# State pass with token rows of two blocks loaded in place of TensorE transposes; last head's PSUM banks and closing weights in another order

## What is computed

```python
proj = x @ w_in                       # split into q_g, k_g, v_g, g_g, gk_lo, q_s, k_s, v_s
gk   = log_sigmoid(gk_lo @ w_gk2 + b_gk) / 16
gla  = gated_linear_attention(q_g, k_g, v_g, gk)   # 4 heads, dk 128, dv 256, recurrent state per head
gla  = rmsnorm(gla) * norm_w * silu(g_g)
swa  = sliding_window_attention(q_s, k_s, v_s, sinks)  # window 128, 16 query heads, 2 kv heads
x    = layer_norm(ALPHA * x + concat(gla, swa) @ w_out)
x    = layer_norm(ALPHA * x + relu(x @ w_up)**2 @ w_down)
```

## Time and profile before

| | us |
|---|---|
| median of 3 executions | 2786.36 (2785.68 to 2789.0) |
| the profiled execution | 2783.01 |
| its span, first to last instruction, slowest core (6) | 2781.5 |
| spans of the eight cores | 2774.0 to 2781.5 |
| granted TensorE clock, mean of a core | 0.995 to 0.998 |
| TensorE busy | 2726.8 |
| DVE, ACT, POOL busy | 1006.6, 601.2, 125.6 |

### The profile page before, as it was taken

One profiled execution on the slowest core, in us unless ns is written; L12 is line 12 of the kernel. 1 busy time (PEld: TensorE's weight loads), 2 busy tenths in 40 slices (PEclk: granted clock), 3 DMA queues, 4 the chain that ended last, 5 costly groups with the idle time before them and its releaser, 6 DMA issues.

```text
span 2781.5 us, 37822 instructions; the slowest of 8 cores (2774.0 to 2781.5 us)
## 1 busy us (share of the span) xinstructions
PE 2726.8 (98%) x14416; PEld 1349.0 (49%) x14416; DVE 1006.6 (36%) x1443; ACT 601.2 (22%) x1247; POOL 125.6 (5%) x227
## 2 busy tenths in 40 slices
PE   7999999999999999999999999999999999999998
PEld 3545773444444444444444676344444444444443
DVE  3643545651212211111248454573211111121248
ACT  3334554231001001001004554332101100100100
POOL 2100000000000000000100000000000000000000
PEclk9999999999999999999999999999999999999999
DMA  9865457534444354444578445734344435444352
GB/s 143 124 97 95 81 100 143 134 80 83 76 76 76 63 89 76 76 67 87 89 123 195 77 83 130 162 84 91 61 87 81 76 61 91 76 76 76 76 107 106
DMA packets 80113, 262.54 MB, mean 94 GB/s; under 512 B 31808, under 2 KB 50752, under 8 KB 51648
## 3 DMA queue, kind: packets, MB, share of 16 engines
q0 software_dynamic: 46320, 211.47, 44.7%
q1 hardware_dynamic: 33616, 48.65, 5.8%
HBM read 448.47 MB, written 16.78 MB: 167 GB/s over the span
## 4 chain that ended last, share of the span: by engine, by line
PE 92%; DVE 2%; ACT 2%; DMA 2%; issue 1%; POOL 0%; DVEq 0%; ACTq 0%; POOLq 0%
PE ps L292 91%; DMA xreg<-w_down 1%; PE ps L295 1%; ACT racc L312 1%; DMA xreg<-xT_prev 1%; ACT rext L312 1%; DVE racc L455 1%; DVE rext L315 0%; DVE racc L323 0%; DVE rexu L315 0%; ACT small L312 0%; DVE S_f L323 0%; DVE racc L315 0%; POOL xreg L335 0%; DVE racc L329 0%
## 5 line engine op out<-in xcount | busy, mean ns | idle before, releaser
L292 PE MATMUL ps<-xreg,wring 128*128 128x512 bf16 (+1 forms) x5568 | 1208.7, 380 | 4.0 <-DVE rexu L323 4.0
L292 PE MATMUL ps<-wring,xreg 128*128 128x512 bf16 (+1 forms) x6432 | 1183.2, 345 | 2.0 <-DVE rexu L323 2.0
L292 PEld LDWEIGHTS ps<-wring,xreg 128*128 128x128 bf16 x6432 | 626.9, 98 | 547.6 <-issue 17.6
L292 PEld LDWEIGHTS ps<-xreg,wring 128*128 128x128 bf16 (+1 forms) x5568 | 539.2, 98 | 650.6 <-issue 16.8
L312 ACT ACTIVATE tmpr<-ps 128x512 f32<-128x512 f32 (+1 forms) x320 | 177.5, 555 | 1423.9 <-PE ps L292 1421.2
L315 DVE TENSOR_TENSOR xreg<-tmpr 128x512 bf16<-128x512 f32 x256 | 177.3, 692 | 703.8 <-ACT tmpr L312 703.8
L315 DVE TENSOR_TENSOR racc<-racc,ps 128x512 f32<-128x512 f32 x240 | 164.7, 687 | 493.2 <-PE ps L292 439.0
L292 PE MATMUL ps<-xreg 128*128 128x512 bf16 (+2 forms) x832 | 176.0, 371 | 3.1 <-DMA xreg<-w_down 3.0
L323 DVE SCALAR_TENSOR_TENSOR racc<-racc,ps 128x512 f32<-128x512 f32 x128 | 87.8, 686 | 220.9 <-PE ps L292 220.9
L323 DVE SCALAR_TENSOR_TENSOR racc<-racc,small,rext 128x2048 f32<-128x2048 f32 (+1 forms) x66 | 149.7, 2274 | 4.6 <-DVE racc L323 2.0
L292 PEld LDWEIGHTS ps<-xreg 128*128 128x128 bf16 x832 | 79.8, 98 | 95.2 <-issue 6.5
(11 more groups left out here) (89 smaller groups left out, 844.5 us busy)
## 6 DMA issues: line engine op xcount, KB each, us to landing
wring<-w_up POOLq DMA_DIRECT2D x64, 1024.0 KB, 9.8
wring<-w_down POOLq DMA_DIRECT2D x60, 1024.0 KB, 9.8
wring<-w_gla POOLq DMA_DIRECT2D x26, 1024.0 KB, 10.0
racc<-x_own SPq DMA_DIRECT2D x16, 1024.0 KB, 13.3
y<-racc SPq DMA_DIRECT2D x15, 1024.0 KB, 4.5
xreg<-xT_prev POOLq DMA_DIRECT2D x16, 512.0 KB, 24.4
xreg<-xT_own POOLq DMA_DIRECT2D x16, 512.0 KB, 17.7
wring<-w_qs POOLq DMA_DIRECT2D x8, 1024.0 KB, 10.5
```

What stands on the lines that cost most here:

```text
L292: P.add("pe", lambda h: h.matmul(out, lhsT=lhsT, rhs=rhs, start=start, stop=stop), [lhsT, rhs], [out])
```

## The change

Six things. A new input `x_prev` holds tokens 512 to 1535 of the earlier half as rows. Blocks 1 and 2 get their token rows from it: `load_rows` issues 4 DMAs on POOL, each 128 rows of 2048. Block 1's go to `x_tok1`, the second half of the weight ring, and are issued after block 2's pieces; block 2's go to `x_tok` and are issued after the sums of block 0. Blocks 0 and 3 are still transposed. The gates of blocks 2 and 3 move to the end of the keys of the block before, ahead of the last head's transposes. The two ring pieces that occupied the second half of the ring (`wcap` 6) are issued after block 1 and not after block 0, behind the first pieces of `xT_own`. In `chunk`, `bu` is taken before `bo`, with the instructions in the old order. The last head's first step (its scores) is advanced before the loop, and the double step at i == 4 goes. In the closing stage quarters 0 and 1 come through the ring, quarters 2 and 3 through `XR`.

```diff
--- before.py
+++ after.py
@@ -188,6 +188,7 @@
     x_own = din("x_own", [NTOK, D])
     xT_own = din("xT_own", [16, 128, 2048])
     xT_prev = din("xT_prev", [16, 128, 2048])
+    x_prev = din("x_prev", [NT, D])
     w_kv = din("w_kv", [128, 4608])
     w_qs = din("w_qs", [4, 128, 4096])
     w_gla = din("w_gla", [12, 128, 4096])
@@ -258,6 +259,7 @@
         x1b = [EY[:, i * 2048:(i + 1) * 2048] for i in range(2)]
         XV = [XR[i][:, :].rearrange("p (k t) -> p k t", k=16) for i in range(2)]
         x_tok = RA[:, 12288:20480].rearrange("p (t e) -> p t e", e=2048)
+        x_tok1 = WR[:, 8192:16384].rearrange("p (t e) -> p t e", e=2048)
         kd_all = [RA[:, 20480 + i * 2048:22528 + i * 2048].rearrange("p (t e) -> p t e", e=512) for i in range(2)]
         kd_tmp = [EY[:, 1024 + i * 512:1536 + i * 512] for i in range(4)]
         wg_prev = EY[:, 3072:3584].rearrange("p (k n) -> p k n", n=32)
@@ -428,6 +430,11 @@
                 issue_x(4)
                 blocks = [XV[1][:, :, 512:1024], XV[1][:, :, 0:512], XV[0][:, :, 0:512], XV[0][:, :, 512:1024]]
 
+                def load_rows(b, dest):
+                    for t in range(4):
+                        lo = (2 - b) * 512 + t * 128
+                        dma("pool", f"r{t}", dest[:, t, :], x_prev[lo:lo + 128, :], [], [dest[:, t, :]])
+
                 def x_rows(b, kg2, tqs=range(4)):
                     for tq in tqs:
                         bkb = next_bank()[:, :].bitcast(BF16)
@@ -477,21 +484,26 @@
                         tt(kd_tmp[h], bk[:, :], tf, ALU.mult)
                         if h:
                             rows(h - 1)
-                    x_rows(b, 1, (3,))
-                    rows(3)
-                    x_rows(b, 1, (2,))
+                    if b in (0, 3):
+                        x_rows(b, 1, (3,))
+                        rows(3)
+                        x_rows(b, 1, (2,))
+                    else:
+                        gates(b + 1)
+                        rows(3)
 
                 def sums(b, dcs):
                     for dc in dcs:
                         bk = next_bank()
                         for t in range(4):
-                            mm(bk[:, :], x_tok[:, t, dc * 128:(dc + 1) * 128], kd_all[b % 2][:, t, :], t == 0, t == 3)
+                            mm(bk[:, :], (x_tok1 if b == 1 else x_tok)[:, t, dc * 128:(dc + 1) * 128], kd_all[b % 2][:, t, :], t == 0, t == 3)
                         mp = m_part[dc // 8][:, dc % 8, :]
                         if b == 0:
                             cp("act" if dc % 2 else "dve", mp, bk[:, :])
                         else:
                             tt(m_all[:, dc, :] if b == 3 else mp, mp, bk[:, :], ALU.add)
 
+                load_rows(1, x_tok1)
                 x_rows(0, 0)
                 gates(0)
                 x_rows(0, 1, (0, 1))
@@ -499,13 +511,17 @@
                 keys(0)
                 for b in range(4):
                     sums(b, range(0, 8))
-                    if b < 3:
-                        x_rows(b + 1, 0)
-                        gates(b + 1)
+                    if b == 2:
+                        x_rows(3, 0)
+                    if b == 0:
+                        gates(1)
                     sums(b, range(8, 16))
+                    if b == 0:
+                        load_rows(2, x_tok)
                     if b < 3:
                         decays(b + 1)
-                        x_rows(b + 1, 1, (0, 1))
+                        if b == 2:
+                            x_rows(3, 1, (0, 1))
                         keys(b + 1)
                     if b == 0:
                         bk = next_bank()
@@ -521,12 +537,12 @@
                         dma("pool", "c6", masks_b[:].rearrange("p a b -> p (a b)"), masks, [], [masks_b[:]])
                         for h in range(2):
                             load_piece(f"wo{h}", wv_prev[h], w_gla[h * 3 + 1])
+                    if b == 1:
+                        queue_half(xT_own, 0, 0, 0, 0)
+                        issue_x(4)
                         wcap[0] = 6
                         if wplan is not None:
                             issue_w()
-                    if b == 1:
-                        queue_half(xT_own, 0, 0, 0, 0)
-                        issue_x(4)
                     if b == 2:
                         wcap[0] = 1 << 30
                         for wi, _ in wks:
@@ -676,10 +692,10 @@
 
                     def chunk(t):
                         half = t // 4
+                        bu = next_bank()
                         bo = next_bank()
                         mm(bo[:, 0:256], At4[half][:, (t % 4) * 128:(t % 4 + 1) * 128], v_tok[hb][:, t, :], True, False)
                         mm(bo[:, 0:256], qtT[hb][:, t * 128:(t + 1) * 128], S_b[:, h, :], False, True)
-                        bu = next_bank()
                         mm(bu[:, 0:256], kd_tok[hb][:, t, :], v_tok[hb][:, t, :], True, True)
                         stt(S_f[:, h, :], S_f[:, h, :], eC[:, h, t:t + 1], bu[:, 0:256], ALU.mult, ALU.add)
                         ss = next_small()
@@ -780,14 +796,13 @@
                 drive(b0)
                 drive(gla_proj(3), (g2, 1.0))
                 drive(g2)
+                advance(g3)
                 for t in range(4):
                     load_res(t)
                 qs1 = swa_proj(1)
                 for i in range(8):
                     advance(qs1)
                     advance(g3)
-                    if i == 4:
-                        advance(g3)
                     if i >= 4:
                         advance(b1)
                         advance(b1)
@@ -974,13 +989,15 @@
 
                     rows = s == 3 and pi == 1
                     early = [[], []]
+                    ahead = []
                     if rows:
+                        ahead = [down_w(0), down_w(1)]
                         for i in range(4):
                             wv = XR[(p + 1) % 2][:, i * 4096:(i + 1) * 4096].rearrange("p (k n) -> p k n", n=512)
-                            load_piece(f"wo{i}", wv, w_down[s * 8 + 2 + i])
+                            load_piece(f"wo{i}", wv, w_down[s * 8 + 4 + i])
                             early[i // 2].append((None, wv))
                     for q in range(1 if rows else 4):
-                        wd = down_w(q)
+                        wd = ahead[0] if rows else down_w(q)
                         issue_x(3)
                         for t in range(8):
                             down_unit(q, t, wd)
@@ -993,12 +1010,12 @@
                         release_w(wd[0][0])
                         release_w(wd[1][0])
                     if rows:
-                        wds = early + [down_w(3)]
+                        wds = [ahead[1]] + early
                         for t in range(8):
                             for i in range(3):
                                 down_unit(1 + i, t, wds[i])
                             ln2_last(t)
-                        for wi, _ in wds[2]:
+                        for wi, _ in wds[0]:
                             release_w(wi)
                 late.extend(lns)
 
@@ -1080,6 +1097,7 @@
         own = xs[b, half * NTOK:(half + 1) * NTOK]
         m["x_own"] = np.ascontiguousarray(own)
         m["xT_own"] = pieces(own)
+        m["x_prev"] = np.ascontiguousarray(xs[b, 0:NT * 3 // 2][NT // 2:]) if half == 1 else np.zeros((NT, D), f)
         m["xT_prev"] = pieces(xs[b, 0:NTOK]) if half == 1 else np.zeros((16, 128, 2048), f)
         prev0 = prev if half == 1 else np.zeros((128, 128), f)
         m["masks"] = np.ascontiguousarray(np.concatenate([causal, cur, prev, prev0], axis=1))
```

## The result

| | before | changed |
|---|---|---|
| executions, us | 2785.68, 2786.36, 2789.00, 2789.19 | 2771.38, 2772.33 |
| the profiled execution | 2783.01 | 2771.38 |
| spans of its eight cores | 2774.0 to 2781.5 | 2762.0 to 2769.8 |
| granted clock, mean of a core | 0.995 to 0.998 | 0.995 to 0.999 |

The ratio is 0.9945, 95% interval [0.9925, 0.9965]: 15.3 us faster, between 10 and 21 (the medians of the listed executions differ by 15.8). The forecast was 2767.9, in a range from 2761 to 2776; the two executions lie 3.5 and 4.4 us above it. Two further executions of the changed kernel, and some of later kernels, had one die at a lower granted clock and were slower, so ratios and medians leave them out, and of the last group's profile of the changed kernel (2787.1 us, one die at a lower clock for part of its length) only cores 0 to 3 are read.

What follows compares the result with a forecast made beforehand. TensorE, busy 98% of the span, was taken to bound the kernel. On core 6, 3.3 + 5.8 + 4.9 + 6.2 = 20.2 us, less 1.7 for a possible clock drop, net 18.5: 2786.4 to 2767.9 us, range 2761 to 2776.

Steps and rivals of the forecast that it cites:

- TensorE's work in the state pass: State pass: transposes removed and gates moved save 3.7 + 0.4 + 2.0 = 6.1 us on TensorE.
- The new wait: Block 1's sums wait 2.8 us, between 2.2 and 3.2, for the fourth row piece, at 3.2 us a piece.
- The rival that the pieces do not overlap: Row pieces one after another: at 8.5 us each 2804 us, chance 0.03; at the skill's 6.15 us 2785, chance 0.02.
- 17% beyond the best rate: Rival for block 1's rows: no wait, no clock drop, 2763.4 us; needs 2.5 us a piece; chance 0.08.
- The clock behind that wait: After block 1's wait for rows, one of eight cores may draw a clock drop: half of 3.4, 1.7 us on top.
- The head: Last head of attention: new bank order and no double chunk save 2.9 us per pass, 5.8 us in two passes.
- a backlog of ACT: Last head, steps 5 to 7: ACT lags 1 us more each step, so 1.9 us stays where 1.3 was.
- The clock in the head: Last head of attention: with less idling both clock drops go, 1.7 + 3.2 = 4.9 us.
- The closing stage: Row stage: the 2.98 us wait for the last closing weights goes, with the 3.2 us clock drop behind it: 6.2 us.
- almost no margin: Closing weights: the last piece is needed 16 matmuls, 3.45 us, later, so its wait goes but only just.
- the clock falls all the same: Rival: the new wait and one attention stretch give a clock drop on the slowest core; 2772.8 us, chance 0.22.
- The order helps less: Rival: ACT binds the last head's steps, each pass gains 1.3 us only, last closing piece late by 1; 2772.1, chance 0.10.

Runs made afterwards that it cites:

- the last group: Three runs on one chip beside the kernel before (2783.0 us): changed kernel again 2770.3, block 1's rows queued ahead of block 2's pieces 2766.0, that plus earlier scores 2766.3.
- state pass alone: The kernel before with only the change's edits to the state pass: 2782.9 us, ratio 0.9992 [0.9974, 1.001].
- closing part: The kernel before with only the change's edit to the closing weights: 2778.5 us, ratio 0.9975 [0.9954, 0.9996].

## Why the prediction was right, and by what it was off

The forecast held in direction and size: 2767.9 against 2771.9 here, and against before -18.5 where this comparison measured -15.3 and the one in the last group -12.6. It held inside the full range; of 2763 to 2771, the forecast's own range without its rivals, it is 0.9 outside. By its own steps:

- **TensorE's work in the state pass: right.** 6.1 us. On core 6, 130.35 - 125.86 = 4.49 gained with a wait of 1.46 inside makes 5.95. The wait on the decayed keys grew from 0.96 to 1.90, by the 0.9 that the gone transposes no longer cover.
- **The new wait: right in price, high on five cores of eight.** 3.25 us a piece against 3.2. The waits were 1.46 to 3.22 in all, median 2.2; the 2.8 assumed block 2's last piece at 69.8, and it came at 68.2 on core 3. The rival that the pieces do not overlap is out at 3.25 us a piece. The Trainium skill (DMA: Bandwidth & Descriptors, "Measured") has 6.15 us for a transfer of 1 MB; laid end to end, as the rival did, that figure does not fit this full queue. The prediction's "17% beyond the best rate" for rows in time is 22% (0.52 MB in 2.5 us is 210 GB/s, against 172).
- **The clock behind that wait: the under-sized term.** I put it at 1.7, as a coin toss for one core. On the chip it is a toss for each of eight, and the slowest core is by nature one that lost it, so it belongs in the sum in full: the drops cost 1.5 to 3.0, and the sum should have been about 17. Of twenty state passes (changed kernel twice, state pass alone; waits of one pass added) the clock fell in none of the seven that waited up to 2.3 us, in two of the five from 2.35 to 2.8, and in all eight from 3.06 up. With two of the eight (3.36 and 4.30) the clock was at the lower level twice as long. The Trainium skill (TensorE: Matmul & The Clock Gate, "HAM oscillation") tells of a kernel in which TensorE waits about 3 to 5 us for a DMA between bursts of matmuls and starts each burst at the lower clock. The eight waits from 3.06 up agree with it; the falls after 2.35 and 2.41 came after shorter waits than it tells of.
- **The head: the bank order works as forecast, the size is off.** Per pass 1.9 and not 2.9. Steps 4 to 7 came out near what was worked: waits of 1.28 (1.0 forecast) and 0.37 + 0.77 + 0.90 = 2.04 (1.9 forecast). The 1.9 is partly luck, for its reason was a backlog of ACT, and in the trace ACT has none: it waits 1.35 us for VectorE in steps 5 and 6, and TensorE's three waits end with VectorE's results. What the sum lacked is the start: scores that are advanced once, directly ahead of the loop, have one projection unit to get through DVE's mask, and the first chunk waits 0.80. I looked at what is removed in step 4 and not at what the moved step waits for. Two passes: 2 us too much.
- **The clock in the head: right.** 1.7 and 3.2 forecast on core 6, 1.7 and 3.2 to 3.3 measured.
- **The closing stage: right.** 6.2 forecast, 6.4 on core 6, and "almost no margin" is borne out: core 0 of the changed kernel waited 0.58 for that piece, and other cores 0.2 to 0.6 in later runs.
- **Missed: 1.0 us** (0.27 + 0.70) of longer ACT waits behind the state pass, cause open.

For core 6 the terms made 20.2 and the trace has 19.5: state pass 1.2 more than forecast, head 1.9 less, closing 0.2 more, 1.0 missed, and 0.7 gained ahead of the first sum. What failed is the step from core 6 to the slowest core. Core 3 ends 7.8 us after it: 2.7 in the state pass (0.95 more wait and a drop of 1.7), 1.7 and 3.7 in the two stretches where its clock was cut with TensorE busy, 0.3 less elsewhere. I had put 1.7 on top for all of this.

The rival "the clock falls all the same", at 2772.8, is half right: at the new wait it fell, in the attention it did not. Its time is 0.9 us from the one measured, by luck in part, since the 5.4 us of core 3's cut clock stand in none of its terms. "The order helps less", at 2772.1, is nearer still and wrong in what it says: the order gained 1.9 a pass and not 1.3, and the last piece was not late by 1.

## What to carry to other kernels

Where work is traded for a transfer, look for its place in the queue before its size: the same four DMAs cost a wait and on half of the cores a clock drop behind block 2's input, and 1.0 us of gates ahead of it. Where the time is that of the slowest of eight cores, an effect that falls on each core with a chance of a half counts in full, and removing what spreads the cores is worth more than its mean (closing part: 3.6 us on the mean core, 5.0 in the time). When a step is pulled ahead, follow what that step feeds: its consumer may now be the first to wait.

## What was not expected of the hardware

- DMAs of half the width (128 rows of 1024 in place of 2048 elements) moved 119 to 133 GB/s where whole ones moved 168 to 172, at the same DMA share: the eight of half size took 2.0 to 2.6 us each and not 1.6.
- Two waits of TensorE of 1.1 and 1.3 us, 3 us apart, brought the clock down in 11 of 16 stretches; without the first of them it was 1 of 16 (over all profiles 56 of 64 and 4 of 136).
- With TensorE busy throughout, all four cores of one die had a granted clock of 0.92 to 0.93 over 40 us while the other die had 1.00, in the same execution; within them it read 0.81, and not the 0.50 that stands behind a wait.
